# Gathered expert rows in up to ten and thirteen places, late sums one slot at a time, and four more query tiles

## The chip, the cores and the metric

The kernel runs on one core of one Trainium2 chip. The metric is the device time of one execution in microseconds (us). The kernel before took 2892.78 us (median of 3 runs, 2888.32 to 2907.57).

## The reference

Two layers of a backbone over 256 latent tokens and 256 context tokens of width 1024, all in float32. Cut to what matters here:

```python
for l in range(2):
    # mixer: pooling, low-rank attention and mLSTM on the context (s=1), then on the latents (s=0)
    mix = concat(pool, attention, mlstm) @ w_out[l];  x = x + g_a * mix
    x = x + g_f * peer_ffn(modulate(x))      # in layer 1 for the latents alone

def peer_ffn(h):                             # blocks of 128 tokens
    q = (h @ w_q)                            # 8 heads, two halves of 128
    s = q . subkeys                          # 128 scores for each half
    top 16 of each half, 256 sums, top 16 of them -> expert (of 16384), g = softmax(best)
    a = gelu(sum_d h[p, d] * u_tab[expert][d])
    y[p] = sum over 8 x 16 experts of (g * a) * v_tab[expert]
```

Each token so reads 128 rows of 8 KB (a row of `u_tab` and one of `v_tab` side by side). That is 512 tokens in the first layer and 256 in the second, 805 MB in all.

## The kernel before

**Phases.** `mixer(0)` is the context mixer of layer 0; `experts(0)` the expert retrieval of the first layer for four tiles of 128 tokens (`TILES`), during which the other work of layer 0 and the start of layer 1 run "behind" it: `mixer(1)` (latents, layer 0), the modulation products of layer 1 (`ada`, from slot 206) and `mixer(2)` (context keys and values of layer 1, from slot 272). Then come `mixer(3)` (latents, layer 1) and `experts(1)` with two tiles.

**Slots.** An expert stage is a row of slots, 128 for each tile of tokens: 512 slots in the first layer and 256 in the second. For slot m GpSimd gathers 128 rows (1 MB) by an indirect DMA (`gather`, L539 to L547). A slot holds 64 tokens twice over: an even slot and the odd one after it serve the two halves of a tile. VectorE multiplies the u half of the slot with the token rows and sums it (`dot`, L1269); ScalarE makes gelu, coefficient and a 128x64 diagonal (`gated`, L844 to L848); TensorE multiplies the diagonal with the v half and adds it into `acc` (`values`, L1660 to L1670). `values` works on a pair of slots: eight matmul instructions that alternate between the upper and lower 64 columns of the array. It counts `v_used` by two at the end of the pair, and `free_pair` (L396) says which count frees a place. There are eight diagonals (`DIAGS`).

**Places.** In the first layer the slots go round the six 1 MB tiles of `fast` (L374), which hold weight tiles in the mixers; in the second round those six and six more in `mix`, the mixers' working memory (L375). Gather m waits until slot m-6 (or m-12) has been summed.

**Queries.** 16 query tiles of 576 KB for each two token tiles (weights and subkeys) come in through `qring`, which has two places; tile n is loaded by SyncE after the scores of tile n-2 (L524 to L528). `query` (L1627) and `key_scores` (L1637) use it. The first eight stand ahead of the slots of a layer; the rest go in parts between them (`query_steps`, L111). The first two heads need the scores of tiles 0 to 3; their indices start the gathers.

**Order.** Each engine runs one list in order. In an expert stage every engine does its part of slot m, and then `Behind.run(m)` (L240) the steps of the other work whose number is at most m. SyncE goes through `ORDER` (L194), loads sorted by a number, each with a wait for the place that it fills: `fast` and `back` (two tiles) for weights, `qring`.

Of the kernel before, what the change touches and what calls it, by code (L numbers as in the profile page):

```python
# [129 lines left out]

QUERIES = [query_steps(e) for e in range(2)]
# [49 lines left out]
def fast_place(n):  # L181
    return n % FAST if n < FIRST_LOADS else (n - FIRST_LOADS + P * len(TILES[0]) - FAST) % FAST
# [11 lines left out]
def load_order():  # L194

    order = []
    for n in range(len(FAST_LOADS)):
        order.append((-2000 + n if n < FIRST_LOADS else 2000 + n, "fast", n))
    for n in range(len(BACK_LOADS)):
        order.append((-500 + n if n < BACK else BACK_LOADS[n - BACK][4], "back", n))  # L200
    for n in range(HC * 3):
        e, u = divmod(n, 2 * HC)
        if n < 2:
            at = -600 + n
        elif n < 2 * HC + 2:
            at = ASKED[0][n - 2] + 2 if n - 2 in ASKED[0] else -400 + n
        else:
            at = 10000 + (ASKED[1][u - 2] if u - 2 in ASKED[1] else -100 + u)
        order.append((at, "query", n))
    order.append((POOLW_AT, "pool", 1))  # L210
    return [o[1:] for o in sorted(order)]
# [53 lines left out]
def build(nc, x_in, c_in, par_in, con_in, w_in, wq_in, uq_in, pw_in, uv_tabs, out):  # L265
    with ExitStack() as ctx:
# [16 lines left out]
        hT = sb("hT", [P, KC, COLS])  # L283
# [56 lines left out]
        W = 7504  # L340
# [8 lines left out]
        modrow2 = part(W, 2, WT)  # L349
# [24 lines left out]
        rings = [[fast[:, s, :] for s in range(FAST)]]  # L374
        rings.append(rings[0] + [part(BIG * s, BIG) for s in range(6)])  # L375

        def slot(e, m):
            return rings[e][m % len(rings[e])]
# [17 lines left out]
        def free_pair(m):  # L396
            return 2 * (m // 2) + 2


# [4 lines left out]
        query_landed = [sem(f"query_landed{i}") for i in range(2)]  # L404
        landed = [sem(f"landed{i}") for i in range(len(rings[1]))]
# [56 lines left out]
        def landings(e, m):  # L462
            n = len(rings[e])
            return 16 * (m // n + 1 + (-(-(P * nts[0] - m % n) // FAST) if e and m % n < FAST else 0))
# [27 lines left out]
        @block.sync  # L492
        def _(sp):
            def load(dst, kind, p, n, landed_):
                if kind == "uq":
                    sp.dma_start(dst[:, 0:UQ_COLS], uq_in[2 * PHASES[p][0] + n]).then_inc(landed_, 16)
                else:
                    sp.dma_start(dst, weight_rows(p, kind, n)).then_inc(landed_, 16)

            sp.dma_start(cT, c_in).then_inc(c_loaded, 16)  # L500
            sp.dma_start(con[:, :], con_in).then_inc(con_loaded, 16)
            for ring, n in ORDER:
                if ring == "fast":
                    p, kind, number = FAST_LOADS[n][:3]
                    if n < FIRST_LOADS:
                        if n >= FAST:
                            done, value = spent(*FAST_LOADS[n - FAST][:3])
                            sp.wait_ge(done.sem, value)
                    elif n < FIRST_LOADS + FAST:
                        m = P * nts[0] - FAST + n - FIRST_LOADS  # L510
                        sp.wait_ge(v_used.sem, v_used.at(0, free_pair(m)))
                    else:
                        done, value = spent(*FAST_LOADS[n - FAST][:3])
                        sp.wait_ge(done.sem, value)
                    s = fast_place(n)
                    load(fast[:, s, :], kind, p, number, fast_landed[s])
                if ring == "back":
                    p, kind, number = BACK_LOADS[n][:3]
                    if n >= BACK:
                        done, value = spent(*BACK_LOADS[n - BACK][:3])  # L520
                        sp.wait_ge(done.sem, value)
                    load(back[:, n % BACK, :], kind, p, number, back_landed[n % BACK])
                if ring == "query":
                    e, u = divmod(n, 2 * HC)  # L524
                    if n >= 2:
                        sp.wait_ge(psc_mm.sem, n - 1)
                    sp.dma_start(qring[:, n % 2, :, :].rearrange("p k c -> p (k c)"),
                                 wq_in[e * HC + u % HC]).then_inc(query_landed[n % 2], 16)  # L528
                if ring == "pool":
                    sp.wait_ge(pool_mm.sem, pool_mm.at(1, 1))  # L530
                    sp.dma_start(poolw[:, :, :], pw_in[1]).then_inc(poolw_loaded, 16)
            sp.wait_ge(x_part.sem, x_part.at(1, 4))
            sp.dma_start(out, xT[:, :, 0:SEQ]).then_inc(s_out, 16)
            sp.wait_ge(s_out, 16)


        @block.gpsimd
        def _(g):
            def gather(e, m):  # L539
                R = len(rings[e])  # L540
                Q, n = divmod(m, QUAD)
                if n < 2:
# [3 lines left out]
                g.indirect_dma_start(slot(e, m), None, uv_tabs[e],  # L546
                                     bass.IndirectOffsetOnAxis(idx[:, Q % 2, n:n + 1], 0)).then_inc(landed[m % R], 16)  # L547
# [8 lines left out]
        def _(a):  # L556
# [32 lines left out]
            def modulate(p, which, k):  # L589
# [3 lines left out]
                h = hT[:, k, cols(p)]  # L593
# [85 lines left out]
            def pooled(p):  # L679
# [4 lines left out]
                for c in range(2):  # L684
                    ins = a.activation(hT[:, c, cols(p)], bank[2][:, c * SEQ:(c + 1) * SEQ], ACT.Copy, scale=par[:, l, PB_PS + c:PB_PS + c + 1])
# [20 lines left out]
            def numbers(p):  # L706
# [13 lines left out]
                a.activation(hT[:, 6:8, cols(p)], bank[3].rearrange("p (c j) -> p c j", c=2), ACT.Copy).then_inc(mt_evac.sem, 1)  # L720
# [118 lines left out]
            def gated(e, m):  # L839
# [6 lines left out]
                if m >= DIAGS:  # L846
                    a.wait_ge(v_used.sem, v_used.at(e, free_pair(m - DIAGS)))
# [62 lines left out]
        def _(v):  # L910
# [52 lines left out]
            def norm1(p):  # L963
                kT, vr, mk, v1 = own(p)
                yield 0
                if p == 0:
                    v.wait_ge(con_loaded, 16)
                    v.wait_ge(loaded, 32)
                if PHASES[p][2]:
# [6 lines left out]
                for k in range(KC):  # L976
                    yield 8 + (k + 1) // 3
                    v.tensor_tensor(hT[:, k, cols(p)], xT[:, k, cols(p)], rms[:, :], ALU.mult).then_inc(hx_ready.sem, 1)
# [178 lines left out]
            def attended(p):  # L1157
                for j in range(8):
# [3 lines left out]
                    v.tensor_copy(hT[:, 2 + c, tile_cols(p, t)], bank[3][:, 0:P]).then_inc(attn_out.sem, 1)  # L1162
# [10 lines left out]
            def norm2(p):  # L1173
# [5 lines left out]
                for k in range(KC):  # L1179
                    yield N2_AT + 1 + (k + 1) // 3  # L1180
                    v.tensor_tensor(hT[:, k, cols(p)], xT[:, k, cols(p)], rms[:, :], ALU.mult).then_inc(hx_ready.sem, 1)
# [80 lines left out]
            def dot(e, m):  # L1262
# [4 lines left out]
                v.wait_ge(landed[m % len(rings[e])], landings(e, m))  # L1267
# [47 lines left out]
        def _(t_):  # L1315
# [69 lines left out]
            def projections(p):  # L1385
                for g, (name, n, tile) in enumerate(groups(p)):
                    first = g == 0 or groups(p)[g - 1][2] != tile
                    for step, (k0, k1) in enumerate(((0, 3), (3, 6), (6, 8))):
# [5 lines left out]
                        for k in range(k0, k1):  # L1394
                            if g == 0:
                                t_.wait_ge(h_ready.sem, h_ready.at(p, k + 1))
                            if name in ("v", "o"):
                                mm = t_.matmul(bank[g % 2][:, 0:WT], hT[:, k, tile_cols(p, n)], w[:, k, :],  # L1398
                                               start=(k == 0), stop=(k == KC - 1))
                            else:  # L1400
# [3 lines left out]
                                mm = t_.matmul(bank[g % 2][0:rows, 0:SEQ], w[:, k, o:o + rows], hT[:, k, cols(p)],  # L1404
# [173 lines left out]
            def out_products(p):  # L1578
                for b in range(KC):
                    for step, (k0, k1) in enumerate(((0, 3), (3, 6), (6, 8))):  # L1580
# [8 lines left out]
                        for k in range(k0, k1):  # L1589
                            mm = t_.matmul(bank[b % 2][:, 0:SEQ], w[:, k, b % 2 * P:b % 2 * P + P], hT[:, k, cols(p)],  # L1590
# [23 lines left out]
            def query(e, u, k0, k1):  # L1614
                n = e * 2 * HC + u
                if k0 == 0:
                    t_.wait_ge(query_landed[n % 2], 16 * (n // 2 + 1))
# [6 lines left out]
                for k in range(k0, k1):  # L1624
                    if u % HC == 0:
                        t_.wait_ge(h_ready.sem, h_ready.at(p, KC + k + 1))
                    mm = t_.matmul(dst[:, 0:SEQ], qring[:, n % 2, k, :], hT[:, k, cols(p)], start=(k == 0), stop=(k == KC - 1))  # L1627
# [3 lines left out]
            def key_scores(e, u):  # L1631
                n = e * 2 * HC + u
# [3 lines left out]
                for j in range(4):  # L1636
                    mm = t_.matmul(b_aside[rows, j * P:(j + 1) * P], pq[:, u % 2, j * HALF:(j + 1) * HALF], qring[:, n % 2, KC, :],  # L1637
# [3 lines left out]
            def rows_turn(e, i, half, f):  # L1641
                o = TILES[e][i] * P + half * HALF
# [4 lines left out]
                for j in range(4):  # L1647
                    for twice in range(2):
                        mm = t_.matmul(b_aside[twice * HALF:(twice + 1) * HALF, j * P:(j + 1) * P], hT[:, 4 * f + j, o:o + HALF], ident,
# [10 lines left out]
            def values(e, m):  # L1660
# [3 lines left out]
                t_.wait_ge(diag_ready.sem, diag_ready.at(e, m + 2))  # L1664
                for f in range(2):
                    for half in range(2):
                        n = m + half
                        mm = t_.matmul(acc[half * HALF:(half + 1) * HALF, f * 512:(f + 1) * 512], diag[:, n % DIAGS, :],  # L1668
                                       slot(e, n)[:, D + f * 512:D + (f + 1) * 512],
                                       start=(n % SLOTS < 2), stop=(n % SLOTS >= SLOTS - 2))  # L1670
                mm.then_inc(v_used.sem, 2)

            def experts(e, behind):
# [13 lines left out]
                for m in range(SLOTS * nt):  # L1687
# [17 lines left out]
                    if m % 2:  # L1705
                        values(e, m - 1)
# [111 lines left out]
```

## Time and profile before

| what | value |
|---|---|
| median of 3 runs | 2892.78 us |
| the profiled execution | 2890.09 us |
| its span (first to last instruction) | 2888.3 us |
| TensorE busy | 2007.8 us, 70% |
| VectorE busy | 1638.7 us, 57% |
| ScalarE busy | 1123.0 us, 39% |
| GpSimd busy (issues of gathers) | 868.1 us, 30% |
| mean granted TensorE clock | 0.83 of 2.4 GHz |
| DMA queue of the gathers | 805.36 MB, 69.1% of 16 engines' span |

How to read it: "busy" is time in which the engine executed an instruction; a stage is read by its own window, since the average of the span mixes stages with different limits. A gather's issue on GpSimd is short; its transfer lands later, on the DMA engines.

### The profile page before, as it was taken

The page shows a single profiled execution, that of the slowest core. Times are in us where ns is not written, and L with a number is a line of the kernel's source. Part 1 is how long each engine was busy: PE and PEld are TensorE (multiplying, and loading weights), DVE is VectorE, ACT ScalarE, POOL GpSimd, SP SyncE. Part 2 cuts the span into 40 slices and gives each one's busy share as a digit, 9 for nine tenths or more (in the row PEclk, how much of TensorE's full clock was granted, in tenths as well). Part 3 has the DMA queues.
Part 4 walks back from the last instruction along what each step waited for, and adds up shares of the span by engine and source line. Part 5 has one row for each costly group of instructions (what it writes and reads, how often), then busy time and mean ns, then how long its engine had stood idle before and what let it go on. Part 6 is the DMA issues. An engine that isn't in the chain of part 4 may idle for free.

```text
span 2888.3 us, 26625 instructions
## 1 busy us (share of the span) xinstructions
PE 2007.8 (70%) x8372; PEld 981.8 (34%) x8372; DVE 1638.7 (57%) x4029; ACT 1123.0 (39%) x3259; POOL 868.1 (30%) x772
## 2 busy tenths in 40 slices
PE   7988598767777777786555555587796865565555
PEld 4756455332343343342111111155574421111111
DVE  2252477668875644676666665432532777776664
ACT  3242263556663433354333333332331443343332
POOL 0000133334354322334344434300001444444442
PEclk9879899878899898898777777786698997787777
DMA  7520499989999999999999999931004999999997
GB/s 311 222 117 17 150 393 412 378 311 372 386 382 411 403 420 421 386 403 394 384 387 369 387 392 391 379 127 46 15 1 154 412 426 426 426 426 426 426 426 303
DMA packets 133660, 940.05 MB, mean 325 GB/s; under 512 B 14864, under 2 KB 16144, under 8 KB 23312
## 3 DMA queue, kind: packets, MB, share of 16 engines
q0 software_dynamic: 110592, 805.36, 69.1%
q1 hardware_dynamic: 22496, 130.31, 11.4%
q10 hardware_dynamic: 432, 2.70, 0.2%
q8 instruction: 66, 1.08, 0.1%
q14 instruction: 74, 0.61, 0.1%
HBM read 937.26 MB, written 1.05 MB: 325 GB/s over the span
## 4 chain that ended last, share of the span: by engine, by line
DMA 42%; PE 32%; DVE 9%; ACT 8%; issue 4%; POOL 4%; POOLq 0%; SPq 0%; DVEq 0%; ACTq 0%
DMA fast<-uv_dram,idx 38%; PE bank L1668 11%; DVE fast L1269 4%; PE bank L1627 4%; PE bank L1404 4%; DMA qring<-wq_dram 3%; POOL fast L546 3%; PE bank L1590 2%; PE bank L1482 2%; ACT diag L848 1%; PE bank L1398 1%; ACT coef L845 1%; PE bank L1637 1%; PE bank L1574 1%; PE bank L1376 1%
## 5 line engine op out<-in xcount | busy, mean ns | idle before, releaser
L546 POOL DMA_INDIRECT fast<-uv_dram,idx x642 | 726.2, 1131 | 1819.4 <-PE bank L1668 1051.9
L1668 PE MATMUL bank<-fast,diag 128*64 128x512 f32 x2568 | 826.7, 777 | 585.7 <-ACT diag L848 585.4
L1269 DVE SCALAR_TENSOR_TENSOR fast<-fast,hrow 128x1024 f32<-128x1024 f32 x642 | 785.8, 1224 | 597.5 <-DMA fast<-uv_dram,idx 590.2
L844 ACT ACTIVATE gact<-araw 128x1 f32<-128x1 f32 x768 | 155.0, 202 | 1089.7 <-DVE fast L1269 922.7
L1668 PEld LDWEIGHTS bank<-fast,diag 128*64 128x64 f32 x2568 | 188.3, 164 | 1110.3 <-ACT diag L848 834.0
L1627 PE MATMUL bank<-hT,qring 128*128 128x256 f32 x768 | 238.7, 443 | 76.6 <-DMA qring<-wq_dram 67.3
L848 ACT ACTIVATE diag<-con,coef 128x64 f32<-128x64 f32 x768 | 267.0, 348 | 25.1
L1668 PE MATMUL bank<-mix,diag 128*64 128x512 f32 x504 | 171.8, 818 | 113.3 <-ACT diag L848 113.3
L845 ACT ACTIVATE coef<-gact,wts 128x1 f32<-128x1 f32 x768 | 226.2, 295 | 24.9
L1627 PEld LDWEIGHTS bank<-hT,qring 128*128 128x128 f32 x768 | 152.2, 215 | 188.0 <-issue 93.6
L1269 DVE SCALAR_TENSOR_TENSOR mix<-mix,hrow 128x1024 f32<-128x1024 f32 x126 | 154.5, 1226 | 98.1 <-DMA mix<-uv_dram,idx 95.2
L546 POOL DMA_INDIRECT mix<-uv_dram,idx x126 | 141.7, 1125 | 161.7 <-PE bank L1668 137.2
L1668 PEld LDWEIGHTS bank<-mix,diag 128*64 128x64 f32 x504 | 38.2, 168 | 235.8 <-ACT diag L848 178.1
L1404 PE MATMUL bank<-hT,back 128*128 128x256 f32 (+1 forms) x336 | 84.0, 389 | 4.1 <-ACT hT L594 4.1
L1404 PE MATMUL bank<-hT,fast 128*128 128x256 f32 (+1 forms) x320 | 76.1, 394 | 4.8 <-ACT hT L594 4.8
L1065 DVE TENSOR_TENSOR mix<-con,bank 128x256 f32<-128x256 f32 x48 | 17.0, 415 | 103.7 <-PE bank L1482 64.0
L1482 PE MATMUL bank<-mix 128*128 128x65 f32 x272 | 54.2, 376 | 30.6 <-DVE mix L1075 30.6
L814 ACT ACTIVATE pq<-bank 128x256 f32<-128x256 f32 x48 | 18.2, 379 | 142.2 <-PE bank L1627 142.1
L1404 PEld LDWEIGHTS bank<-hT,back 128*128 128x128 f32 (+1 forms) x336 | 63.3, 190 | 17.9 <-issue 7.4
L844 ACT ACT_TABLE_LOAD x52 | 66.7, 1283 | 0.9
L1404 PEld LDWEIGHTS bank<-hT,fast 128*128 128x128 f32 (+1 forms) x320 | 61.1, 194 | 16.6 <-issue 7.3
L1482 PEld LDWEIGHTS bank<-mix 128*128 128x128 f32 x272 | 50.9, 286 | 42.3 <-issue 42.3
(222 smaller groups left out, 2337.4 us busy)
## 6 DMA issues: line engine op xcount, KB each, us to landing
fast<-w_dram SPq DMA_DIRECT2D x48, 1024.0 KB, 7.2
back<-w_dram SPq DMA_DIRECT2D x44, 1024.0 KB, 9.9
qring<-wq_dram SPq DMA_DIRECT2D x48, 576.0 KB, 8.2
fast<-uv_dram,idx POOLq DMA_INDIRECT x642, 9.9
fast<-uq_dram SPq DMA_DIRECT2D x4, 576.0 KB, 4.4
xT<-x_dram ACTq DMA_DIRECT2D x1, 2048.0 KB, 8.7
mix<-uv_dram,idx POOLq DMA_INDIRECT x126, 22.2
back<-uq_dram SPq DMA_DIRECT2D x2, 576.0 KB, 8.2
```

The costliest lines, as they stand in the source:

```text
L546: g.indirect_dma_start(slot(e, m), None, uv_tabs[e], bass.IndirectOffsetOnAxis(idx[:, Q % 2, n:n + 1], 0)).then_inc(landed[m % R], 16)
L844: link(a.activation(gact[:, n:n + 1], araw[:, Q % 2, n:n + 1], ACT.Gelu))
L845: link(a.activation(coef[:, n:n + 1], gact[:, n:n + 1], ACT.Copy, scale=wts[:, Q % 2, n:n + 1]))
L848: a.activation(diag[:, m % DIAGS, :], two, ACT.Copy, scale=coef[:, n:n + 1]).then_inc(diag_ready.sem, 1)
L1269: v.scalar_tensor_tensor(out=u, in0=u, scalar=1.0, in1=hrow[:, (2 * i + half) % 3, :], op0=ALU.mult, op1=ALU.mult, accum_out=araw[:, Q % 2 ...
L1376: t_.matmul(bank[3][:, 0:SEQ], ones, sq[:, n % 2, :], start=first, stop=last).then_inc(sq_used.sem, 1)
L1398: mm = t_.matmul(bank[g % 2][:, 0:WT], hT[:, k, tile_cols(p, n)], w[:, k, :], start=(k == 0), stop=(k == KC - 1))
L1404: mm = t_.matmul(bank[g % 2][0:rows, 0:SEQ], w[:, k, o:o + rows], hT[:, k, cols(p)], start=(k == 0), stop=(k == KC - 1))
L1482: mm = t_.matmul(bank[3][:, o:o + MD + 1], mE[:, e, kc, q * P:(q + 1) * P], v1[:, kc % 2, h, :], start=(kc == kcs[0]), stop=(kc == kcs[-1]))
L1590: mm = t_.matmul(bank[b % 2][:, 0:SEQ], w[:, k, b % 2 * P:b % 2 * P + P], hT[:, k, cols(p)], start=(k == 0), stop=(k == KC - 1))
L1627: mm = t_.matmul(dst[:, 0:SEQ], qring[:, n % 2, k, :], hT[:, k, cols(p)], start=(k == 0), stop=(k == KC - 1))
L1668: mm = t_.matmul(acc[half * HALF:(half + 1) * HALF, f * 512:(f + 1) * 512], diag[:, n % DIAGS, :], slot(e, n)[:, D + f * 512:D + (f + 1) * ...
```

## The change

It touches four things.

1. **Places by table.** `ring_table` gives each slot the least recently used of the places open to it. First layer: the six `fast` tiles always; the context half of `hT` (now stored as its own 1 MB) for slots 134 to 265 and again from 312; the tile of `mix` at 5448 from slot 180; two tiles at 7504 and 9552 for slots 180 to 261 and again from 336. So six places to slot 133, seven to 179, ten to 261, seven or eight to 335, ten after that. Second layer: six `fast`, the context half of `hT`, six of `mix`: thirteen. The first gather into an opened place waits for the mixer's last use of it (`opening`), and the mixers wait before they write there again.
2. **Single slots.** `values(e, m, n)` sums n slots. Slots from 336 in the first layer and all of the second (`SINGLE`) are summed alone: four matmul instructions on one half of the columns, `v_used` counted by one.
3. **Query tiles.** Tiles 2 to 5 of each layer go to four places of their own in `mix` (`more_q`), loaded as soon as the attention ahead is done; tiles 6 and 7 follow the scores of tiles 0 and 1. From tile 8 on the two places are used as before.
4. **What goes with it.** The rows of the layer-1 modulation move in `mix`; weight tiles of `mixer(3)` take the `fast` places in the order in which their last gathers fall.

```diff
+MIX_W = 7504
+FAST_USES = [[("fast", s, 0, P * n, None) for s in range(FAST)] for n in (4, 2)]
+USES = (FAST_USES[0] + [("ctx", 0, 134, 266, "turned"), ("ctx", 0, 312, 512, "projected"),
+                        ("mix", 5448, 180, 512, "attended"), ("mix", MIX_W, 180, 262, "attended"), ("mix", MIX_W + BIG, 180, 262, "attended"),
+                        ("mix", MIX_W, 336, 512, "rows"), ("mix", MIX_W + BIG, 336, 512, "rows")],
+        FAST_USES[1] + [("ctx", 0, 0, 256, None)] + [("mix", BIG * s, 0, 256, None if s < 3 else "asked") for s in range(6)])
+SECOND_FREE = 266
+SINGLE = (336, 0)
+
+def ring_table(e):
+    last, table = {}, []
+    for m in range(P * len(TILES[e])):
+        use = min((u for u in USES[e] if u[2] <= m < u[3]), key=lambda u: last.get(u, -1))
+        table.append((use[0:2], last.get(use), use[4]))
+        last[use] = m
+    return table
+
+def freed(e, m):
+    return m + 1 if m >= SINGLE[e] else 2 * (m // 2) + 2
...
-        hT = sb("hT", [P, KC, COLS])
+        hT = sb("hT", [P, 2, KC, SEQ])
...
-        modrow2 = part(W, 2, WT)
+        modrow2 = part(W + 4608, 2, WT)
...
+        more_q = part(W, 4, KC + 1, P)
+        def query_tile(e, u):
+            return more_q[:, u - 2, :, :] if 2 <= u < 6 else qring[:, u % 2, :, :]
...
+        def opening(e, what):
+            if what == "turned":
+                return hr_ready, hr_ready.at(0, 8)
+            if what == "projected":
+                return in_mm, in_mm.at(2, len(groups(2)))
+            if what == "attended":
+                return out_mm, out_mm.at(1, 1)
+            if what == "rows":
+                return tr_evac, tr_evac.at(2, 2 * len(items(2)))
+            return psc_mm, psc_mm.at(1, 6)
...
-                    if n >= 2:
-                        sp.wait_ge(psc_mm.sem, n - 1)
+                    if 2 <= u < 6:
+                        sp.wait_ge(attn_out.sem, attn_out.at(3 * e, 8))
+                    elif u in (6, 7):
+                        sp.wait_ge(psc_mm.sem, psc_mm.at(e, u - 5))
+                    elif u >= 8:
+                        sp.wait_ge(psc_mm.sem, psc_mm.at(e, u - 1))
+                    elif e:
+                        sp.wait_ge(psc_mm.sem, psc_mm.at(0, 2 * HC - 1 + u))
...
-                if m >= R:
-                    g.wait_ge(v_used.sem, v_used.at(e, free_pair(m - R)))
+                if before is not None:
+                    g.wait_ge(v_used.sem, v_used.at(e, freed(e, before)))
+                elif first:
+                    done, value = opening(e, first)
+                    g.wait_ge(done.sem, value)
...
+                if p == 1:
+                    v.wait_ge(psc_mm.sem, psc_mm.at(0, 6))
+                if p == 2:
+                    v.wait_ge(v_used.sem, v_used.at(0, freed(0, SECOND_FREE - 1)))
...
-            def values(e, m):
+            def values(e, m, n):
...
-                t_.wait_ge(diag_ready.sem, diag_ready.at(e, m + 2))
+                t_.wait_ge(diag_ready.sem, diag_ready.at(e, m + n))
                 for f in range(2):
-                    for half in range(2):
-                        n = m + half
-                        mm = t_.matmul(acc[half * HALF:(half + 1) * HALF, f * 512:(f + 1) * 512], diag[:, n % DIAGS, :],
-                                       slot(e, n)[:, D + f * 512:D + (f + 1) * 512],
-                                       start=(n % SLOTS < 2), stop=(n % SLOTS >= SLOTS - 2))
-                mm.then_inc(v_used.sem, 2)
+                    for j in range(m, m + n):
+                        half = slice(j % 2 * HALF, j % 2 * HALF + HALF)
+                        mm = t_.matmul(acc[half, f * 512:(f + 1) * 512], diag[:, j % DIAGS, :], slot(e, j)[:, D + f * 512:D + (f + 1) * 512],
+                                       start=(j % SLOTS < 2), stop=(j % SLOTS >= SLOTS - 2))
+                mm.then_inc(v_used.sem, n)
...
-                    if m % 2:
-                        values(e, m - 1)
+                    if m >= SINGLE[e]:
+                        values(e, m, 1)
+                    elif m % 2:
+                        values(e, m - 1, 2)
```

## Rows read from the trace of the kernel before

**Rows 1.** Busy time by stretch; the x of POOL counts the gathers issued.

```profile
263.00:356.00 93.00, 58.47 (x275) 44.18 (x276) 28.25 (x105) 19.09 (x46) 7.03 (x7) 0.82 0.33 119
356.00:756.00 400.00, 313.28 (x1300) 160.06 (x1299) 280.85 (x685) 216.47 (x579) 144.66 (x128) 0.88 0.94 373
756.00:880.00 124.00, 98.53 (x491) 52.86 (x491) 102.44 (x279) 78.22 (x202) 57.91 (x46) 0.98 0.98 382
880.00:1177.00 297.00, 221.60 (x1214) 104.93 (x1213) 149.09 (x361) 106.32 (x334) 88.70 (x83) 0.89 1.00 411
1177.00:1322.00 145.00, 118.11 (x486) 60.55 (x485) 102.86 (x263) 69.53 (x208) 56.30 (x51) 0.93 0.99 396
1322.00:1392.00 70.00, 43.17 (x127) 11.96 (x126) 46.98 (x109) 35.13 (x98) 28.63 (x24) 0.78 1.00 395
1392.00:1872.00 480.00, 258.50 (x770) 61.14 (x772) 291.17 (x682) 165.43 (x547) 193.66 (x176) 0.75 0.98 384
2255.00:2848.00 593.00, 371.90 (x1212) 106.21 (x1208) 404.22 (x971) 230.45 (x769) 274.58 (x241) 0.79 1.01 425
```

The columns are the window, its length, then busy us and count of PE, PEld, DVE, ACT and POOL, the granted clock, the DMA share and GB/s.

**Rows 2.** Waits from 1400 to 1860 us: in total, times, longest.

```profile
POOL fast L546 <- PE bank L1668: 250.1, 83, 7.4
DVE fast L1269 <- DMA fast<-uv_dram,idx: 175.1, 158, 3.6
```

**Rows 3.** Gathers over the whole run: issue to landing, least, median, most.

```profile
DMA to landing us min/median/max: 5.4/10.5/25.2
```

**Rows 4.** Timeline, start of the first expert stage: start, us, engine, line, operation.

```profile
271.75 1.09 PE L1637 MATMUL bank<-qring,pq 128*64 128x128 f32 x8
276.27 5.41 PE L1627 MATMUL bank<-hT,qring 128*128 128x256 f32 x16 [3.44 <-DMA qring<-wq_dram]
301.68 1.09 PE L1637 MATMUL bank<-qring,pq 128*64 128x128 f32 x8
303.50 1.09 PE L1649 MATMUL bank<-con,hT 128*64 128x128 f32 x16 [0.74 <-ACT keysB L826]
309.90 3.72 PE L1627 MATMUL bank<-hT,qring 128*128 128x256 f32 x16
313.76 1.08 POOL L546 DMA_INDIRECT fast<-uv_dram,idx  x1 [313.31 <-DVE idx L1238]
322.77 2.00 POOL L546 DMA_INDIRECT fast<-uv_dram,idx  x1 [7.94 <-DVE idx L1238]
336.77 6.01 PE L1627 MATMUL bank<-hT,qring 128*128 128x256 f32 x16 [9.41 <-DMA qring<-wq_dram]
342.71 1.09 PE L1637 MATMUL bank<-qring,pq 128*64 128x128 f32 x8
352.14 3.38 PE L1668 MATMUL bank<-fast,diag 128*64 128x512 f32 x8 [2.62 <-ACT diag L848]
355.81 1.61 POOL L546 DMA_INDIRECT fast<-uv_dram,idx  x1 [26.06 <-PE bank L1668]
```

**Rows 5.** Timeline, start of the second expert stage.

```profile
2168.47 1.09 PE L1637 MATMUL bank<-qring,pq 128*64 128x128 f32 x8
2196.79 1.09 PE L1637 MATMUL bank<-qring,pq 128*64 128x128 f32 x8
2217.88 2.00 POOL L546 DMA_INDIRECT fast<-uv_dram,idx  x1 [8.22 <-DVE idx L1238]
```

**Rows 6.** Timeline: a pair of slots at either clock, and the last of stage one.

```profile
1699.66 1.92 PE L1668 MATMUL bank<-fast,diag 128*64 128x512 f32 x4
1703.22 3.68 PE L1668 MATMUL bank<-fast,diag 128*64 128x512 f32 x8 [1.64 <-ACT diag L848]
1708.49 1.94 PE L1668 MATMUL bank<-fast,diag 128*64 128x512 f32 x8 [1.59 <-ACT diag L848]
1873.62 17.18 SPq L498 DMA_DIRECT2D fast<-w_dram  x6
```

**Rows 7.** Waits of PE over the whole run.

```profile
PE bank L1627 <- DMA qring<-wq_dram: 67.3, 17, 9.4
```

**Rows 8.** The page's DMA issues: KB each where known, median us from issue to landing.

```profile
fast<-uv_dram,idx POOLq DMA_INDIRECT x642, 9.9
mix<-uv_dram,idx POOLq DMA_INDIRECT x126, 22.2
```

**Rows 9.** Waits for weight tiles from 880 to 1177 us.

```profile
PEld bank L1342 <- DMA back<-w_dram: 0.4, 1, 0.4
```

More of the change, by code:

```diff
@@ L128, in query_steps, with last_gather @@
     return steps
+MIX_W = 7504
[13 more added lines that the diff above has]
+    return table
+RINGS = [ring_table(e) for e in range(2)]
+def freed(e, m):
+    return m + 1 if m >= SINGLE[e] else 2 * (m // 2) + 2
+def last_gather(place):
+    return max(m for m, entry in enumerate(RINGS[0]) if entry[0] == place)
+FAST_ORDER = sorted(range(FAST), key=lambda s: last_gather(("fast", s)))
 QUERIES = [query_steps(e) for e in range(2)]
@@ L200, in load_order @@
         order.append((-500 + n if n < BACK else BACK_LOADS[n - BACK][4], "back", n))
[L201 to L209, printed above, removed]
+    for e in range(DEPTH):
+        for u in range(HC * len(STREAMS[e])):
+            if u < 2:
+                at = -600 + u if e == 0 else ASKED[0][2 * HC - 2 + u] + 2
+            elif u < 10:
+                at = 10000 * e - 400 + u
+            else:
+                at = 10000 * e + ASKED[e][u - 2] + 2
+            order.append((at, "query", (e, u)))
     order.append((POOLW_AT, "pool", 1))
-    return [o[1:] for o in sorted(order)]
+    return [o[1:] for o in sorted(order, key=lambda o: o[0])]
 ORDER = load_order()
@@ L403, in build @@
         back_landed = [sem(f"back_landed{i}") for i in range(BACK)]
-        query_landed = [sem(f"query_landed{i}") for i in range(2)]
-        landed = [sem(f"landed{i}") for i in range(len(rings[1]))]
+        query_landed = [sem(f"query_landed{i}") for i in range(6)]
+        places = sorted({entry[0] for table in RINGS for entry in table})
+        landed = {place: sem(f"landed_{place[0]}{place[1]}") for place in places}
         cs_clear, cs_ready, s_out = sem("cs_clear"), sem("cs_ready"), sem("s_out")
@@ L460, in build @@
         y_ready, yt_mm, x_part = signal("y_ready", *each(1)), signal("yt_mm", *each(2)), signal("x_part", *each(2))
-        def landings(e, m):
-            n = len(rings[e])
-            return 16 * (m // n + 1 + (-(-(P * nts[0] - m % n) // FAST) if e and m % n < FAST else 0))
+        landings, counts = [], {place: 0 for place in places}
+        for table in RINGS:
+            landings.append([])
+            for entry in table:
+                counts[entry[0]] += 16
+                landings[-1].append(counts[entry[0]])
+        query_counts, counts = {}, [0] * 6
+        for e, u in [n for kind, n in ORDER if kind == "query"]:
+            s = u if 2 <= u < 6 else u % 2
+            counts[s] += 16
+            query_counts[(e, u)] = (query_landed[s], counts[s])
+        def opening(e, what):
[8 more added lines that the diff above has]
+            return psc_mm, psc_mm.at(1, 6)
         def spent(p, kind, n):
```

66 lines of the change are left out of this document (34 added, 32 removed).

## The prediction

> **What bounds the kernel now.** I read the busy time by stretch first [rows 1]. The cuts at 756, 880, 1177, 1322, 1392 and 1872 us are the issues of gathers 134, 180, 262, 312, 336 and 511; the counts of POOL show it (7 and 128 issues up to 756 us, one at each cut counted twice). In the second expert stage, with twelve places, the transfers run at 425 GB/s and 241 gathers take 593 us, 2.46 us each. That is the rate of the transfers alone: nothing else in the trace moves more. In the first stage, with six places, no stretch reaches it: 382, 411, 396, 395 and 384 GB/s. The clearest is 1392 to 1872 us, where nothing runs behind the slots: 176 gathers in 480 us, 2.73 us each, though TensorE is busy for 54% only. Then the waits of that stretch [rows 2]: GpSimd waits for the sums (250.1 us), VectorE for the landing rows (175.1 us). It is a closed loop of six places, 6 x 2.73 = 16.4 us round; a gather takes 5.4 us to land at best, 10.5 in the median [rows 3]. More places lengthen the loop's allowance without lengthening its work.
>
> Last the two starts [rows 4, 5]. Each of the tiles 2 to 7 is fetched only after the scores of the tile two before it, and TensorE waits for it, 3.44 to 9.41 us at a time [rows 4]; 67.3 us in all [rows 7]. The DMA engines do little meanwhile (119 GB/s from 263 to 356 us [rows 1]), and the gathers wait for the scores of tile 3.
>
> **Query tiles, first layer.** With tiles 2 to 5 there, TensorE goes from the scores at 271.75 us by 3.72 us of query, 1.09 of scores and some 0.35 between, 5.2 us a tile, so the scores of tile 3 fall at 287.3 instead of 301.68: 14.4 us. The first gather moves from 313.76 to 299.4, the second from 322.77 to 308.4. From the scores of tile 3 to query 5 lie the row turns, 8.2 us (301.68 to 309.90), so query 5 begins at 295.5 and the scores of tile 6 at about 310 instead of 342.71. The first sum at 352.14 came 9.4 us after those; but the second gather must land too (308.4 and some 9 us, then 3 for dot, diagonal and start), and tile 8 is now fetched beside gathers. I put the first sum at 321.5 us, 30.6 us earlier, and gather 6, which waits for it, 30 us earlier [rows 4]. From there TensorE's list of slots and mixer steps is the same. **Term 30 us**; bounds 14 (only the first gather's shift survives) and 33. Four tiles are fetched during the output products of the mixer, where the DMA engines are all but idle; their wait on SyncE's queue has only query loads behind it that are needed later, so it costs nothing. The new wait of VectorE in norm1 of `mixer(1)`, for the scores of tile 5 at about 305 us, sits behind the first dot and the weights' wait, both later than 310: nothing.
>
> **Slots 6 to 133**: six places, as before; nothing.
>
> **Slots 134 to 335**: at 425 GB/s the four stretches would give (1-382/425) x 124 + (1-411/425) x 297 + (1-396/425) x 145 + (1-395/425) x 70 = 12.5 + 9.8 + 9.9 + 4.9 = 37 us [rows 1]. Places are seven, ten, seven or eight there, and TensorE has the mixer and the modulation products in its list (busy 75 to 81% up to 1322 us), so weight tiles and engines take turns as the limit. I take half, **19 us**; bounds 0 and 38. The new waits of GpSimd for an opened place fall ahead of use: "attended" is the first output product at step 169, and slots 180 to 182 would have waited for sums 174 and later; the others are 5 to 12 slots early likewise. VectorE's wait before `mixer(2)` asks at slot 272 for the sum of slot 265; with diagonals running a few slots behind it costs 0 to 3 us, once.
>
> **Slots 336 to 511**: ten places. The loop may now take 24.6 us at 2.46 us a slot against the 16.4 measured, so the transfers set the pace: 176 x (2.73 - 2.46) = 47 us; one off for weight tiles of `mixer(3)`, three of which now start while nine gathers are still out instead of two with four. **Term 46**; bounds 10 (the DMA engines were busy 0.98 of this stretch already) and 49.
>
> **Single slots.** The price is on TensorE. A pair takes 1.94 us at 2.4 GHz and 3.68 at 1.2 GHz [rows 6]. The halves of a pair run side by side: 16 instructions of 64 columns that alternate between halves take 1.09 us, eight that stay in one half also 1.09 [rows 4]. So a single slot, four instructions in one half, costs as much as a pair, some 1.75 us back to back at 2.4 GHz and 3.45 at 1.2: 432 slots now demand 71% of the time at the upper level, against 39% before, and more than all of it at the lower. Before, the granted clock was 0.98 where TensorE was busy for 79% (756 to 880 us), 0.93 at 81%, and 0.75 where it was busy for 54% in short bursts [rows 1]. Singles keep it busy for over 70%, so I take a clock above 0.9 and no loss. The Trainium skill ("TensorE: Matmul & The Clock Gate", Part 3) says that matmuls of under 128 output columns should go to distinct column groups to run side by side; the rows agree that singles give that up, and by that rule alone TensorE's time on these slots would double. It says too (Part 1) that activity releases the clock gate, by which the doubling would pay for itself here; no row here shows singles.
>
> **Second layer.** The scores of tile 3 fall at 2168.47 + 3 x 5.2 = 2184 instead of 2196.79, so the train of gathers starts 12.7 us before 2217.88 [rows 5]. The stage is bound by transfers from there on, so the shift carries to the end. Tile 7 no longer is fetched within it (1.4 us) and the hole about 2255 us, where twelve gathers were in before the first sum, nearly closes (2 us). Against that, in the first 16 slots TensorE has 1.75 + 0.93 (query) + 0.36 (scores) = 3.0 us a slot against 2.8 us of transfers, which thirteen places mostly cover: 2 us lost. At the end the last sum takes 1.9 instead of 3.6 us, in both layers: 2 us. **Term 16**; bounds 8 and 21.
>
> **Sum**: 30 + 19 + 46 + 16 = 111 us. The profiled execution took 2890.1 us (a span of 2888.3 and 1.8 around it), 2.7 under the median of the runs; 2890 - 111 = 2779, and against the median 2782. I say **2780 us**. Ends of all terms together: 32 and 141, so 2858 and 2749.
>
> **Rivals.**
> - *The transfers are already full* in the first stage: DMA shares of 0.98 to 1.00 speak for it, and 384 against 425 GB/s at nearly the same share against it. Then slots 134 to 511 give some 12 us instead of 65: 2890 - 30 - 12 - 16 = 2832. Chance 0.10.
> - *Full rate everywhere from slot 134*, and both starts at their best: 33 + 38 + 49 + 21 = 141, so 2749. For it: 411 GB/s is reached in the richest stretch with only six places. Chance 0.12.
> - *Gathers crowd out the weight tiles.* In 880 to 1177 us TensorE takes a modulation tile every two slots from two `back` places; with ten gathers queued each tile lands later, and the slots behind it stall. For it: gathers land after 22.2 us in the added places of the second layer against 9.9 mostly with six [rows 8]. Against: gathers were nearly always out already, and in this stretch TensorE waited for a tile once, 0.4 us [rows 9]. The middle would lose 15 us instead of gaining 19: 2814. Chance 0.07.
> - *Slower: single slots run at 1.2 GHz.* No row shows long runs on half of the columns; were the lower level granted in them, a slot takes 3.45 us, and 432 slots take 1490 us instead of the present 480 + 630: +380 less the 30 + 19 + 16 that remain, about 3205 us. It decides when the mean clock of those stretches is under 0.71 (1.75 / 0.71 = 2.46) and makes the whole slower than before under some 0.64 (111 / 432 = 0.26 us more a slot). Against: at 1.2 GHz TensorE would never pause, and the rows have the lower clock only beside pauses. Chance 0.04.
>
> **Numbers.** My forecast holds 0.67 (2758 to 2808 its own range). The range 2748 to 2838 takes in the first three rivals for the most part and leaves out the last. A change of under 1% (29 us) can't be told from none. Faster by over 1% are the forecast and the first three rivals but for a sliver: 0.94; within 1%: 0.02; slower: 0.04.
>
> **What would show it.** After the change: first gather at about 299 us and gather 6 near 326; tiles 2 to 5 with no DMA wait; 2.46 us a slot and 420 GB/s or more from slot 336 on, with a clock over 0.9 and TensorE busy for over 70%; the first train of layer two 12.7 us sooner after the scores of tile 0. Wrong would be: a slot rate of 2.6 or more from 336 (first rival), a mean clock of under 0.75 there (the last), new waits of TensorE for `back` (the third).

## The result: 2788 us against 2894, faster by 3.7%

The changed kernel took 2788.48 us (median of 4 runs, 2785.47 to 2790.81), the kernel before, with one more run beside it, 2893.71 us. The ratio is 0.9626, 95% interval 0.9604 to 0.9648. Predicted were 2780 us, range 2748 to 2838. Executions of one kernel within one comparison differ by 4 to 23 us; some 10 us of that is traced below, between profiles, to the granted clock of one stretch.

The profiled execution of the changed kernel took 2789.06 us with a span of 2787.3, 101.0 us under the span before. Busy time by stretch, with cuts at the issues of the same gathers as in [rows 1] (columns as there):

```profile
263.00:326.00 63.00, 48.71 (x272) 37.31 (x272) 29.54 (x104) 20.69 (x49) 6.82 (x6) 0.94 0.32 118
326.00:729.00 403.00, 317.62 (x1294) 163.51 (x1292) 278.57 (x674) 210.66 (x570) 142.54 (x129) 0.86 0.93 369
729.00:851.00 122.00, 98.84 (x489) 52.18 (x490) 104.48 (x290) 82.14 (x208) 57.00 (x47) 0.97 0.99 393
851.00:1129.00 278.00, 208.71 (x1166) 98.86 (x1164) 142.43 (x343) 99.95 (x315) 90.24 (x82) 0.91 1.01 421
1129.00:1282.00 153.00, 127.08 (x532) 67.12 (x532) 111.02 (x286) 75.75 (x227) 57.45 (x51) 0.92 1.01 416
1282.00:1346.00 64.00, 40.85 (x124) 12.03 (x126) 43.55 (x97) 33.96 (x94) 28.35 (x24) 0.78 1.01 421
1346.00:1780.00 434.00, 330.40 (x769) 84.42 (x766) 288.27 (x686) 163.33 (x539) 172.31 (x177) 0.99 1.01 421
2140.00:2745.00 605.00, 494.19 (x1212) 140.78 (x1211) 408.93 (x983) 230.30 (x770) 242.07 (x242) 1.00 1.01 425
```

What to see: from 851 us on the transfers run at 416 to 421 GB/s where they ran at 384 to 411; the last stretch of the first layer has a granted clock of 0.99 instead of 0.75 and TensorE busy for 76% instead of 54%; the second layer keeps its 425 GB/s and goes from 0.79 to 1.00.

The start of the first expert stage in the timeline, answering to [rows 4]:

```profile
275.78 1.09 PE L1712 MATMUL bank<-qring,pq 128*64 128x128 f32 x8
276.80 3.72 PE L1703 MATMUL bank<-hT,mix 128*128 128x256 f32 x16
289.78 1.09 PE L1712 MATMUL bank<-mix,pq 128*64 128x128 f32 x8
301.86 1.07 POOL L619 DMA_INDIRECT fast<-uv_dram,idx  x1 [301.41 <-DVE idx L1315]
322.58 3.68 PE L1744 MATMUL bank<-fast,diag 128*64 128x512 f32 x8 [4.45 <-ACT diag L921]
326.54 1.78 POOL L619 DMA_INDIRECT fast<-uv_dram,idx  x1 [8.71 <-PE bank L1744]
```

The queries of tiles 2 to 7 follow with no wait for a tile. From the scores of tile 0 to those of tile 3 it is 14.0 us instead of 29.9, and gather 6 goes out at 326.54 instead of 355.81.

Waits of PE over the run, answering to [rows 7], and single slots late in the second layer, answering to the pair of [rows 6]:

```profile
PE bank L1703 <- DMA qring<-wq_dram: 9.5, 6, 2.2
```

```profile
2501.51 1.93 PE L1744 MATMUL bank<-fast,diag 128*64 128x512 f32 x4 [0.56 <-ACT diag L921]
2504.00 1.93 PE L1744 MATMUL bank<-fast,diag 128*64 128x512 f32 x4 [0.56 <-ACT diag L921]
2506.48 1.93 PE L1744 MATMUL bank<-fast,diag 128*64 128x512 f32 x4 [0.55 <-ACT diag L921]
```

Four instructions of a single slot take 1.93 us, the same as the eight of a pair; the engine then idles for only 0.56 us.

**By stage.** An issue shows when a place came free, not when its rows arrived, and the two drift apart as the queue deepens. So all kernels are compared by the start of the dot of a slot in the timeline (VectorE's line 1269 before, 1346 in the change), counted from slot 0. "T0" and "T0'" are the scores of tile 0 of layers one and two; in brackets the us at 1.2 GHz within slots 64 to 95, from the granted clock. All in us:

| kernel | T0 | T0 to slot 6 | 6 to 134 | 134 to 336 | 336 to 504 (a slot) | 504 to 511 | 511 to T0' | T0' to 525 | 525 to 767 |
|---|---|---|---|---|---|---|---|---|---|
| before | 271.7 | 90.3 | 401.1 (48) | 640.1 | 458.7 (2.731) | 22.0 | 284.4 | 97.6 | 605.9 |
| the change | 275.8 | 57.9 | 408.1 (70) | 618.3 | 422.3 (2.514) | 24.8 | 280.1 | 76.2 | 608.9 |
| queries_only | 274.3 | 58.0 | 413.5 (72) | 642.9 | 464.2 (2.763) | 21.9 | 282.5 | 77.5 | 607.1 |
| queries_singles | 278.5 | 57.7 | 401.0 (49) | 641.8 | 420.8 (2.505) | 21.7 | 282.4 | 76.1 | 608.4 |
| all_pairs | 277.2 | 58.0 | 402.7 (54) | 619.2 | 422.3 (2.513) | 24.8 | 281.2 | 77.6 | 607.0 |
| places_singles | 273.6 | 88.5 | 402.2 (52) | 620.1 | 422.2 (2.513) | 24.7 | 280.9 | 97.6 | 607.3 |
| early_places | 277.2 | 58.0 | 414.6 (72) | 619.4 | 422.4 (2.515) | 21.7 | 285.7 | 76.4 | 608.3 |
| singles_134 | 277.0 | 59.0 | 401.1 (55) | 648.0 | 422.2 (2.513) | 24.8 | 280.5 | 76.1 | 608.9 |
| held_weights | 273.7 | 58.0 | 398.4 (51) | 620.5 | 420.6 (2.504) | 17.3 | 279.8 | 76.3 | 608.6 |
| pairs_held | 274.8 | 58.0 | 402.0 (54) | 621.3 | 420.8 (2.505) | 17.3 | 281.9 | 77.5 | 607.4 |
| change_again | 270.3 | 58.0 | 399.2 (48) | 619.9 | 422.2 (2.513) | 24.8 | 280.5 | 76.2 | 608.6 |
| held_again | 274.2 | 58.0 | 405.8 (62) | 620.0 | 422.3 (2.514) | 17.3 | 281.2 | 76.1 | 608.8 |

After the dot of slot 767 came 16.3 us before and 14.7 in the change.

### The profile page after: what moved, and what is told of

It reads as the page before. It is cut to its first block, busy times and chain, and to the rows that moved or that the text cites. A ratio compares the mean times of both kernels' runs of the same rounds, so it can differ in the third digit from the quotient of the medians.

```text
span 2787.3 us, 26625 instructions
## 1 busy us (share of the span) xinstructions
PE 2209.2 (79%) x8372; PEld 1037.6 (37%) x8372; DVE 1639.0 (59%) x4029; ACT 1121.3 (40%) x3259; POOL 813.1 (29%) x772
## 4 chain that ended last, share of the span: by engine, by line
DMA 45%; PE 31%; DVE 10%; ACT 10%; issue 3%; POOL 1%; SPq 0%; DVEq 0%; POOLq 0%; ACTq 0%
DMA fast<-uv_dram,idx 28%; DMA mix<-uv_dram,idx 16%; PE bank L1744 10%; PE bank L1703 4%; PE bank L1481 4%; DVE fast L1346 3%; PE bank L1667 2%; PE bank L1559 2%; ACT diag L921 1%; PE bank L1475 1%; ACT coef L918 1%; PE bank L1537 1%; PE bank L1651 1%; PE bank L1712 1%; ACT L917 1%
## 5 line engine op out<-in xcount | busy, mean ns | idle before, releaser
L619 POOL DMA_INDIRECT fast<-uv_dram,idx x506 | 544.2, 1075 | 1497.5 <-PE bank L1744 778.5
L1346 DVE SCALAR_TENSOR_TENSOR fast<-fast,hrow 128x1024 f32<-128x1024 f32 x506 | 619.3, 1225 | 407.7 <-DMA fast<-uv_dram,idx 401.2
L1744 PE MATMUL bank<-mix,diag 128*64 128x512 f32 x820 | 387.9, 630 | 120.9 <-ACT diag L921 119.3
L1346 DVE SCALAR_TENSOR_TENSOR mix<-mix,hrow 128x1024 f32<-128x1024 f32 x205 | 251.4, 1226 | 194.7 <-DMA mix<-uv_dram,idx 192.3
L619 POOL DMA_INDIRECT mix<-uv_dram,idx x205 | 206.4, 1007 | 327.5 <-PE bank L1744 306.1
L1744 PEld LDWEIGHTS bank<-mix,diag 128*64 128x64 f32 x820 | 93.7, 140 | 370.0 <-ACT diag L921 250.3
L1703 PE MATMUL bank<-hT,qring 128*128 128x256 f32 x640 | 196.3, 425 | 17.7 <-DMA qring<-wq_dram 9.5
L1744 PE MATMUL bank<-hT,diag 128*64 128x512 f32 x228 | 117.4, 640 | 39.8 <-ACT diag L921 39.8
L1346 DVE SCALAR_TENSOR_TENSOR hT<-hT,hrow 128x1024 f32<-128x1024 f32 x57 | 69.8, 1225 | 50.5 <-DMA hT<-uv_dram,idx 50.5
L619 POOL DMA_INDIRECT hT<-uv_dram,idx x57 | 62.4, 1094 | 107.5 <-PE bank L1744 104.9
L1744 PEld LDWEIGHTS bank<-hT,diag 128*64 128x64 f32 x228 | 27.7, 142 | 113.2 <-ACT diag L921 77.5
```

The source lines that it names most:

```text
L619: g.indirect_dma_start(slot(e, m), None, uv_tabs[e], bass.IndirectOffsetOnAxis(idx[:, Q % 2, n:n + 1], 0)).then_inc(landed[place], 16)
L1346: v.scalar_tensor_tensor(out=u, in0=u, scalar=1.0, in1=hrow[:, (2 * i + half) % 3, :], op0=ALU.mult, op1=ALU.mult, accum_out=araw[:, Q % 2 ...
L1703: mm = t_.matmul(dst[:, 0:SEQ], query_tile(e, u)[:, k, :], own_h(p)[:, k, :], start=(k == 0), stop=(k == KC - 1))
L1744: mm = t_.matmul(acc[half, f * 512:(f + 1) * 512], diag[:, j % DIAGS, :], slot(e, j)[:, D + f * 512:D + (f + 1) * 512], start=(j % SLOTS < ...
```

## The experiments

The theory at this point: three separate gains, each with a cause of its own (query tiles for the starts, added places for the transfers from slot 134 on, single slots as a help that costs nothing). The rival: single slots, not places, fill the late stretch, or the other way round.

### The query tiles alone (queries_only)

```diff
-USES = (FAST_USES[0] + [("ctx", ...), ...], FAST_USES[1] + [("ctx", 0, 0, 256, None)] + [...])
+USES = (FAST_USES[0], FAST_USES[1] + [...])          # six and twelve places
-SINGLE = (336, 0)
+SINGLE = (512, 256)                                  # pairs throughout
```

> The query tiles alone: places as before (six, twelve), pairs throughout. My account: the two starts carry 28 us and 16 us and nothing else does, so 2893 - 44 = about 2849 us, with 2.73 us a slot from slot 336 and a clock of about 0.75 there. Rival (the new places, not the query tiles, made the starts earlier, since gather 6 waited for the first sum): under 20 us gained, above 2873.

Measured 2850.07 us, ratio 0.9849 (0.9807 to 0.9891). The starts take 58.0 and 77.5 us, as in the change (57.9 and 76.2); slots 134 to 336 and 336 to 504 are no shorter than before (642.9 and 464.2 us against 640.1 and 458.7). The account holds, and the rival falls. Its late stretch:

```profile
1389.00:1853.00 464.00, 260.64 (x744) 61.73 (x742) 279.28 (x656) 158.88 (x524) 184.84 (x168) 0.72 0.98 379
```

### Query tiles and single slots, six and twelve places (queries_singles)

```diff
-USES = (FAST_USES[0] + [("ctx", ...), ...], FAST_USES[1] + [("ctx", 0, 0, 256, None)] + [...])
+USES = (FAST_USES[0], FAST_USES[1] + [...])          # SINGLE stays (336, 0)
```

> Query tiles and single slots, but six and twelve places as before. Account A (only the number of places sets the late rate): 2.73 us a slot from 336, as with the query tiles alone, 2849 us. Account B (a single slot shortens the loop of six places as well, by half a slot of waiting and the higher clock, 16.4 us to about 14.5): 2.5 to 2.6 us a slot from 336, so 25 to 40 us less, 2810 to 2825. In the second layer no difference.

Measured 2802.89 us, ratio 0.9682 (0.9638 to 0.9725). Account A falls, account B holds, and by more than it said: 2.505 us a slot from 336, with six places. The window of that stretch, and who waits in it:

```profile
1379.00:1800.00 421.00, 322.14 (x742) 82.64 (x743) 279.03 (x656) 159.09 (x524) 165.95 (x169) 1.00 1.01 420
```

```profile
POOL fast L617 <- PE bank L1742: 248.1, 157, 3.5
DVE fast L1344 <- DMA fast<-uv_dram,idx: 141.1, 156, 2.2
PE bank L1742 <- ACT diag L919: 97.5, 154, 2.5
```

GpSimd waits for nearly every sum (157 times, 3.5 us at most, against 83 times and up to 7.4 in [rows 2]), and still the transfers run at 420 GB/s. The six places now go round in 6 x 2.505 = 15.0 us instead of 16.4, and they are no longer the limit: with ten places and single slots the change is no faster (2.514 us a slot). Two things shorten the round, that each place is freed by its own sum and that the sums run at the higher clock (1.93 us each, where a pair took 1.94 or 3.68); no run tells the two apart. From slot 134 to 336, where pairs stand and places stay six, nothing is gained: 641.8 us.

### All places, pairs throughout (all_pairs)

```diff
-SINGLE = (336, 0)
+SINGLE = (512, 256)
```

> The change with all its places and query tiles, but pairs throughout. My account: with ten and thirteen places the transfers set the pace either way, so the time stays within 5 us of the change (2784 to 2794), with a clock back at about 0.75 in the late stretches. Rival (single slots are what pays late): 2.6 us a slot or more from 336, 2810 us or more.

Measured 2784.73 us, ratio 0.9624 (0.9582 to 0.9665): the same as the change. The late stretch of the first layer and the second layer:

```profile
1357.00:1779.00 422.00, 241.13 (x744) 57.63 (x742) 279.44 (x655) 158.84 (x524) 179.46 (x167) 0.77 1.01 421
2163.00:2770.00 607.00, 358.76 (x1160) 96.35 (x1158) 405.33 (x961) 232.38 (x769) 263.36 (x232) 0.80 1.00 421
```

The clock is back at 0.77 and TensorE at 57%, and the rate is the same 2.513 us a slot. With this and the run above the late stretch is settled: **either** four more places **or** single slots fill it, and the second of them adds nothing.

### Places and single slots, queries as before (places_singles)

```diff
-            return more_q[:, u - 2, :, :] if 2 <= u < 6 else qring[:, u % 2, :, :]
+            return qring[:, u % 2, :, :]
...
-                    if 2 <= u < 6:
-                        sp.wait_ge(attn_out.sem, attn_out.at(3 * e, 8))
-                    elif u in (6, 7):
-                        sp.wait_ge(psc_mm.sem, psc_mm.at(e, u - 5))
-                    elif u >= 8:
+                    if u >= 2:
                         sp.wait_ge(psc_mm.sem, psc_mm.at(e, u - 1))
```

> The change without its query tiles: places by table and single slots, tiles 2 to 7 again through two places. My account: the starts go back, the rest stays: 2788 + 28 + 15 = 2831 us. Rival (the early start is partly paid back by later waits, or the places alone start earlier): under 2815 us.

Measured 2834.83 us, ratio 0.9802 (0.9758 to 0.9847), as the account has it. The starts are those of before (88.5 and 97.6 us against 90.3 and 97.6), the rest is the change. By the medians the query tiles cost 46 us when taken away here and gave 43 when added alone. By the table both starts together are worth 52 us in either case (88.5 + 97.6 against 57.9 + 76.2, and 90.3 + 97.6 against 58.0 + 77.5), of which 1 to 2 us are paid back after slot 525. The rest of the difference lies within what executions of one kernel differ by.

### Added places only up to slot 335 (early_places)

```diff
-("ctx", 0, 312, 512, "projected"), ("mix", 5448, 180, 512, "attended"), ...
-("mix", MIX_W, 336, 512, "rows"), ("mix", MIX_W + BIG, 336, 512, "rows")
+("ctx", 0, 312, 336, "projected"), ("mix", 5448, 180, 336, "attended"), ...
```

> The change with its added places for slots 134 to 335 alone; from 336 on six places and single slots. After the run with six places and singles (2.505 us a slot late) I expect the late places to be worth nothing beside single slots: 2788 us within 4, with 2.50 to 2.52 us a slot. Rival (ten places are needed once the stretch begins behind the mixer): 2795 us or more.

Measured 2784.43 us over 6 runs, ratio 0.9609 (0.9585 to 0.9632): no loss. 2.515 us a slot late, and 619.4 us from 134 to 336. The late places are worth nothing for the rate beside single slots. In the profile, slots 504 to 511 take 3.1 us less than in the change and the mixer after them 5.6 more; the medians don't show it. Its profiled execution was a long one, 2800.31 us, with 72 us at 1.2 GHz in slots 64 to 95.

### Single slots from 134 on (singles_134)

```diff
-SINGLE = (336, 0)
+SINGLE = (134, 0)
```

> The change with single slots from slot 134 on instead of 336. TensorE was busy for 475 of 617 us from slot 134 to 335; 202 singles add some 0.9 us each at 2.4 GHz, 180 us, so it needs 655 us. My account: that stretch is 40 to 60 us longer, 2830 to 2850 us. Rival (earlier freed places and a higher clock pay for it): 2788 us or less.

Measured 2810.95 us, ratio 0.9699 (0.9671 to 0.9727), so slower than the change, but by less than I said: slots 134 to 336 take 648.0 us, 30 more. The waits are those from 729 to 1370 us:

```profile
747.00:1395.00 648.00, 595.48 (x2283) 252.85 (x2282) 396.40 (x1002) 280.90 (x835) 222.66 (x207) 0.99 0.99 396
```

```profile
PE bank L1744 <- ACT diag L921: 48.0, 38, 3.5
```

TensorE is busy for 92% at a clock of 0.99 and waits for diagonals for 48 us in all: here it is the bound. My 655 us of need left out what the clock gives back: it was 0.78 to 0.97 in these stretches with pairs. So the price of a single, 0.9 us of TensorE, is real, and where the engine has other work it is paid.

### Weight tiles held back at the end of the first layer (held_weights, pairs_held)

The first six tiles of the last mixer wait for the sum of slot 509 instead of the last one in their place.

```diff
-                        sp.wait_ge(v_used.sem, v_used.at(0, freed(0, m)))
+                        sp.wait_ge(v_used.sem, v_used.at(0, max(freed(0, m), 510)))
```

> The change, but the first six weight tiles of the last mixer wait until slot 509 is summed. In the change three of them (7.4 us of transfers) go between the last gathers of the first layer: the last four dots come 3 to 5 us apart instead of 2.5. My account: the last dot comes 6 to 7 us sooner, and the mixer, which needs its first such tile some 30 us later, doesn't feel it: 2782 us, 6 less. Rival (the tiles are then late, or the transfers were not in the way): no gain, or a new wait of TensorE for a weight tile after the stage.

> All places and query tiles, pairs throughout, and the same held tiles. If the two are independent: 2785 - 6 = 2779 us, the fastest so far. If pairs lose at a colder clock once the stage ends sooner: 2784 or more.

Measured 2779.71 us (ratio 0.9601, 0.9578 to 0.9623) and, with pairs throughout, 2777.62 us (0.9595, 0.9567 to 0.9622). In the timeline of the change the dots of the last slots come after the tiles begin:

```profile
1781.70 30.07 SPq L562 DMA_DIRECT2D fast<-w_dram  x6
1782.47 1.22 DVE L1346 SCALAR_TENSOR_TENSOR fast<-fast,hrow 128x1024 f32<-128x1024 f32 x1 [1.25 <-DMA fast<-uv_dram,idx]
1784.97 1.22 DVE L1346 SCALAR_TENSOR_TENSOR mix<-mix,hrow 128x1024 f32<-128x1024 f32 x1 [1.26 <-DMA mix<-uv_dram,idx]
1789.32 1.23 DVE L1346 SCALAR_TENSOR_TENSOR mix<-mix,hrow 128x1024 f32<-128x1024 f32 x1 [3.12 <-DMA mix<-uv_dram,idx]
1794.29 1.22 DVE L1346 SCALAR_TENSOR_TENSOR mix<-mix,hrow 128x1024 f32<-128x1024 f32 x1 [3.73 <-DMA mix<-uv_dram,idx]
1799.22 1.23 DVE L1346 SCALAR_TENSOR_TENSOR hT<-hT,hrow 128x1024 f32<-128x1024 f32 x1 [3.69 <-DMA hT<-uv_dram,idx]
```

and in that of held_weights:

```profile
1781.13 1.23 DVE L1346 SCALAR_TENSOR_TENSOR hT<-hT,hrow 128x1024 f32<-128x1024 f32 x1 [1.26 <-DMA hT<-uv_dram,idx]
1783.61 1.23 DVE L1346 SCALAR_TENSOR_TENSOR fast<-fast,hrow 128x1024 f32<-128x1024 f32 x1 [1.24 <-DMA fast<-uv_dram,idx]
1786.02 1.22 DVE L1346 SCALAR_TENSOR_TENSOR fast<-fast,hrow 128x1024 f32<-128x1024 f32 x1 [1.18 <-DMA fast<-uv_dram,idx]
1787.80 5.21 SPq L562 DMA_DIRECT2D fast<-w_dram  x6
1788.48 1.22 DVE L1346 SCALAR_TENSOR_TENSOR fast<-fast,hrow 128x1024 f32<-128x1024 f32 x1 [1.23 <-DMA fast<-uv_dram,idx]
```

Three dots come 4.4 to 5.0 us after the one ahead in the first, all 2.5 or less in the second: slots 504 to 511 in 17.3 us instead of 24.8, and the mixer after it is hardly longer (279.8 against 280.1 us; with pairs 281.9 against 281.2). That is a gain of 7.5 us in the stage.

### The change and the held tiles on one chip (change_again, held_again)

> The change itself once more, beside the next kernel on one chip. Slots 64 to 95 hold the same work in every kernel so far and took 105 us with 48 to 54 us of them at 1.2 GHz in five profiles, 114 to 116 us with some 70 us in the others; I expect one of these two again, whichever the clock gives, and 2788 us in the median. Rival (that difference comes with the change's places or its earlier start): 114 us again.

> The held weight tiles beside the change on one chip. 6 to 8 us less than it: 2781 us against 2788; slots 504 to 511 in 17.3 us against 24.8. Rival (the nine microseconds between the medians so far were chips and clock): within 3 us of the change.

Measured 2780.24 us (2776.17 to 2786.72, ratio 0.9610, 0.9589 to 0.9631) and 2779.80 us (2778.89 to 2787.56, ratio 0.9605, 0.9584 to 0.9625). The stage gain is there again in the profile (24.8 against 17.3 us), but the medians are equal: the rival's wording, within 3 us, is met. The profiled executions say why it can hide. The change had a lucky one: scores of tile 0 at 270.3 us against 274.2, and slots 6 to 133 in 399.2 us against 405.8, of which slots 64 to 95 in 104.4 against 109.7. Whether the 7.5 us show in the median is left open. The change's own second measurement shows that it varies by some 8 us from one comparison to the next (2788.48, 2780.24), so the held tiles are not shown to beat it.

The same run answers on slots 64 to 95. The changed kernel took 114.2 us for them once and 104.4 the second time, with the same instructions:

```profile
517.00:631.00 114.00, 81.19 (x286) 38.48 (x287) 71.94 (x175) 54.00 (x144) 36.68 (x33) 0.69 0.77 294
```

against its second profile and the kernel before:

```profile
511.70:616.10 104.40, 69.48 (x282) 32.00 (x280) 72.10 (x174) 53.32 (x143) 37.97 (x33) 0.77 0.86 319
544.00:649.00 105.00, 72.13 (x282) 34.10 (x280) 71.78 (x174) 53.08 (x142) 35.60 (x32) 0.77 0.84 317
```

The work is the same, the granted clock is 0.69 against 0.77. The whole difference is time in which TensorE is busy (81.2 us against 69.5 and 72.1); it idles for 33 to 35 us in all three. Over all profiles the stretch took 104 to 106 us with 48 to 55 us of it at 1.2 GHz, 110 with 62, and 114 to 116 with 70 to 72. The rival, that the change brings this, falls. Why the clock was granted otherwise in one execution than in the next stays open.

## Why the prediction was right, point by point

- **Query tiles, first layer** (30 us, bounds 14 and 33): right. From T0 to the dot of slot 6 it is 32.4 us less. The tiles come 4.67 us apart, not 5.2.
- **Slots 6 to 133** (nothing): right for the change, wrong for this profile. It lost 7.0 us there and 4.1 us before T0. Neither is the change's: its second profile has 399.2 us there and T0 at 270.3. TensorE is busy for 319.8 us in slots 6 to 133 against 314.3 before and 309.0 in the second profile, and before T0 for 232.7 against 228.7 and 226.7, with the same instructions.
- **Slots 134 to 335** (19 us, half of what the rate allows): 21.8 us by the dots. That it is the places is shown: 640 to 643 us in the three kernels with six, 618 to 621 with the added ones and pairs, whatever else they have.
- **Slots 336 to 511** (46 us): the mechanism held, the size was off; 33.6 us. The term was mis-sized by its floor: I took 2.46 us a slot, from counting issues in the second layer. By its dots that layer ran at 605.9 / 242 = 2.50 us a slot, with its query tiles, and every kernel that fills the late stretch of the first has 2.50 to 2.52. The issues had run ahead: from the issue of a gather to its dot it was 12.7 us at slot 525 and 23.7 us at slot 767, and 11.0 / 242 = 0.05 us a slot is what counting them left out. On 168 slots that is 9 us, with the 0.01 us by which the first layer is slower on the average. Another 2.8 us went to the weight tiles between the last gathers, where I had set one.
- **Why the late stretch fills**: the step "ten places, so the transfers set the pace" is true but not the whole cause. I gave all 46 us to places and none to single slots. Single slots with six places do the same (2.505 us a slot). Had the change had only one of the two, my working would have missed by 38 us for single slots alone (458.7 against 420.8).
- **Single slots**: the price and the clock came out as argued. A single costs 1.93 us where a pair costs 1.94; the sums keep TensorE busy for 1217.5 us in all against 998.5 before and 974.8 with pairs throughout; the clock went to 0.99 and 1.00 in both stretches. The rival of slots at 1.2 GHz, about 3205 us, is refuted. The Trainium skill's advice to put small matmuls on distinct column groups ("TensorE: Matmul & The Clock Gate", Part 3) agrees with this trace on the cost. Here the cost decides only where TensorE has no time to spare, as from slot 134 (30 us lost), and not where the transfers bound the stage.
- **Second layer** (16 us): from T0' to slot 767 it is 18.4 us less, 21.4 at the start and 3.0 given back after slot 525. The second gather goes out 35.1 us after T0' instead of 49.4, so 14.3 us sooner, not 12.7. Of what is given back, early query tiles bring 1.1 to 1.5 us by themselves (607.0 to 607.4 us with pairs against 605.9), single slots without them 1.4 (607.3), and both together 2.4 to 3.0; why was not tried. The tail is 1.6 us shorter, but not through single slots, as I had it: the last sum took 3.57 us before and 1.93 in the change, and all three kernels with early tiles and pairs end with a pair in 1.94 us and the same tail of 14.7. The last pair before ran at the lower clock, theirs at the upper. The thirteenth place has no part in it: with twelve, queries_singles has the same 76.1 and 608.4 us.
- **The mixer between** (nothing said): 4.3 us less, of which 1.7 are the last sum; it is 279.8 to 285.7 us in the other profiles, so no more than that is the change's.
- **Sum**: 32.4 - 4.1 - 7.0 + 21.8 + 33.6 + 4.3 + 18.4 + 1.6 = 101.0 us, the whole of the difference. That the forecast of 111 came so near is in part luck: the late stretch gave 12 us less than its term and the clock of this profile took 11, while the other stages gave some 13 more than theirs. The first rival (transfers full already) falls by 421 against 384 GB/s, the second (full rate everywhere) is met in part in the middle (21.8 of 37 us: 393 GB/s from 729 to 851 us, 416 to 421 after that), the third (weight tiles crowded out) is not seen there (two waits for a `back` tile, 0.8 us in all, from 851 to 1282 us), but its mechanism stands at the end of the stage, the other way round: there weight tiles crowd the gathers.

## What to carry to other kernels

Look at places and the time that each is held together: in this loop, short of places, freeing each one sooner (2.505 us a slot) was worth as much as adding four (2.513), and the second of the two remedies added nothing once the transfers were full. Before counting a gain at the rate of another stage, measure that rate by when data is used, not by when it is asked for. Look at the last transfers of a stage: here the prefetch that its freed buffers set off went between them.

## What the runs showed of the hardware that was not expected

- The same instructions took 104.4 and 114.2 us (slots 64 to 95) in two executions of one kernel, with 48 and 70 us of it at 1.2 GHz. TensorE was busy there for some 70%, in short pieces with pauses between. So one profile differed from another by 10 us with no cause in the code.
- Full transfers run at 420 to 422 GB/s in the first layer and at 424 to 426 in the second; by the dots it is 2.517 us a slot in slots 360 to 480 and 2.489 in slots 620 to 740, with no query tile loaded in either. The page of the change has it in its 40 slices of 69.7 us; why they differ by 1% was not tried:

```profile
GB/s 316 235 123 36 217 404 406 358 275 393 395 387 421 421 420 421 412 420 421 422 421 421 421 421 421 372 71 30 16 37 242 424 425 426 425 426 426 426 426 309
```
